# Second attention's output and the query projections as three rounded products, and late inputs split from the PSUM banks

## What is computed

```python
# first block, layer 0: differential attention, layer 1: stick-breaking attention
for i in range(DEPTH):
    h = rms_norm(x, norm1_g[i]) * (1.0 + sc1) + sh1
    y = diff_attention(h, ...) if i % 2 == 0 else stick_breaking_attention(h, sb_w_in, sb_w_out)
    x = x + g1 * y
    h = rms_norm(x, norm2_g[i]) * (1.0 + sc2) + sh2
    x = x + g2 * hierarchical_moe(h, ...)          # 32 experts, two for each token
x = rms_norm(x, final_norm_g)

def stick_breaking_attention(h, w_in, w_out):
...
    o = jnp.concatenate(outs, axis=1)
    return o.reshape(B, S, D) @ w_out

# second block, two layers
for l in range(DEPTH):
    h = h + hybrid_mixer(rms_norm_2(h, norm_mix[l]), ..., w_in[l], ..., w_out[l])
    h = h + memory_cross_attention(rms_norm_2(h, norm_xattn[l]), mem, norm_mem[l], wq[l], wk[l], wv[l], wo[l])

def memory_cross_attention(hn, mem, norm_mem, wq, wk, wv, wo):
    q = (hn @ wq).reshape(B, S, MEM_HEADS, MEM_HEAD_DIM)
    k = (memn @ wk).reshape(B, M, MEM_HEADS, MEM_HEAD_DIM)
...
    return o @ wo
```

## Time and the profile before

| | us |
|---|---|
| median of 3 runs | 2563.96 (2563.16 to 2566.67) |
| profiled execution, device time | 2564.52 |
| its span | 2562.7 |
| PE busy in it | 2279.2 (89%) |
| DVE busy | 1139.8 (44%) |
| ACT busy | 612.6 (24%) |
| POOL busy | 304.7 (12%) |
| mean granted TensorE clock | 0.951 of full speed |
| moved by DMA | 587.05 MB, mean 229 GB/s |

### The profile page before, as it was taken

One profiled execution on the slowest core, in us unless ns is written; L12 is line 12 of the kernel. 1 busy time (PEld: TensorE's weight loads), 2 busy tenths in 40 slices (PEclk: granted clock), 3 DMA queues, 4 the chain that ended last, 5 costly groups with the idle time before them and its releaser, 6 DMA issues.

```text
span 2562.7 us, 35298 instructions
## 1 busy us (share of the span) xinstructions
PE 2279.2 (89%) x13248; PEld 1517.4 (59%) x13248; DVE 1139.8 (44%) x2035; ACT 612.6 (24%) x1247; POOL 304.7 (12%) x555
## 2 busy tenths in 40 slices
PE   5988786999989869998799998985998999998997
PEld 3874464565545448654456454544786767786765
DVE  3236745334333342473533333335338525228615
ACT  3224520000000032461000000003336125226213
POOL 0001001222122210000122212221000000001000
PEclk8999897999999989999799999998999799999799
DMA  6247757999999942214799999994220021211021
GB/s 253 99 164 323 284 229 288 418 419 418 416 420 377 418 182 92 77 62 166 296 420 419 419 415 419 369 418 164 91 87 34 1 115 44 99 55 66 1 82 42
DMA packets 129177, 587.05 MB, mean 229 GB/s; under 512 B 28008, under 2 KB 28170, under 8 KB 72474
## 3 DMA queue, kind: packets, MB, share of 16 engines
q1 hardware_dynamic: 116704, 566.44, 55.2%
q0 software_dynamic: 12064, 16.87, 1.8%
q10 hardware_dynamic: 288, 2.10, 0.2%
HBM read 580.04 MB, written 27.30 MB: 237 GB/s over the span
## 4 chain that ended last, share of the span: by engine, by line
PE 70%; DVE 12%; DMA 12%; ACT 3%; issue 2%; POOL 1%; SPq 0%; DVEq 0%; ACTq 0%
PE banks L1397 15%; PE banks L1179 9%; PE banks L1180 9%; PE banks L1181 9%; PE banks L1415 8%; DMA normed_by_feature<-in_expert_w_up 6%; PE banks L1332 2%; PE banks L1210 2%; DVE normed_by_token L2344 2%; PE banks L1378 1%; PE banks L1101 1%; DMA scratch<-in_ada_w 1%; DMA weight_ring<-in_expert_w_up 1%; DMA weight_ring<-in_sb_w_in 1%; PE banks L1425 1%
## 5 line engine op out<-in xcount | busy, mean ns | idle before, releaser
L1397 PE MATMUL banks<-weight_ring,scratch 128*64 128x256 f32 x3328 | 381.5, 383 | 27.1 <-DMA weight_ring<-in_expert_w_gate 13.7
L1397 PEld LDWEIGHTS banks<-weight_ring,scratch 128*64 128x64 f32 x3328 | 238.9, 138 | 189.0 <-issue 53.9
L1179 PE MATMUL banks<-weight_ring_rounded,scratch_rounded 128*128 128x512 f32 x768 | 304.2, 396 | 8.3 <-DVE ormed_by_feature_rounded L2181 5.2
L1181 PE MATMUL banks<-weight_ring_rounded,scratch_rounded 128*128 128x512 f32 x768 | 300.6, 391 | 0.0
L1180 PE MATMUL banks<-weight_ring_rounded,ormed_by_feature_rounded 128*128 128x512 f32 x768 | 300.5, 391 | 0.0
L2168 DVE TENSOR_TENSOR weight_ring_rounded<-weight_ring,weight_ring_rounded 128x4096 fp32r<-128x4096 f32 x26 | 115.0, 4424 | 228.5 <-ACT weight_ring_rounded L1669 228.5
L1179 PEld LDWEIGHTS banks<-weight_ring_rounded,scratch_rounded 128*128 128x128 f32 x768 | 145.0, 189 | 47.1 <-issue 9.9
L1181 PEld LDWEIGHTS banks<-weight_ring_rounded,scratch_rounded 128*128 128x128 f32 x768 | 145.1, 189 | 30.8
L1415 PE MATMUL banks<-normed_by_token,scratch 128*64 128x512 f32 x640 | 146.1, 598 | 18.5 <-ACT scratch L1867 18.5
L1180 PEld LDWEIGHTS banks<-weight_ring_rounded,ormed_by_feature_rounded 128*128 128x128 f32 x768 | 145.1, 189 | 28.6
L1397 PE MATMUL banks<-normed_by_feature,scratch 128*64 128x256 f32 x1280 | 147.6, 381 | 15.9 <-DMA normed_by_feature<-in_expert_w_up 15.9
(11 more groups left out here) (391 smaller groups left out, 3437.0 us busy)
## 6 DMA issues: line engine op xcount, KB each, us to landing
weight_ring<-in_expert_w_gate SPq DMA_DIRECT2D x128, 1024.0 KB, 18.4
weight_ring<-in_expert_w_up SPq DMA_DIRECT2D x64, 1024.0 KB, 20.2
weight_ring<-in_expert_w_down SPq DMA_DIRECT2D x64, 1024.0 KB, 20.8
normed_by_feature<-in_expert_w_up SPq DMA_DIRECT2D x64, 1024.0 KB, 19.0
normed_by_token<-in_expert_w_down SPq DMA_DIRECT2D x64, 1024.0 KB, 19.1
weight_ring<-in_ada_w SPq DMA_DIRECT2D x20, 2048.0 KB, 12.1
weight_ring<-in_w_in SPq DMA_DIRECT2D x12, 2048.0 KB, 8.0
weight_ring<-in_diff_w_in SPq DMA_DIRECT2D x6, 2048.0 KB, 8.1
```

The costliest lines, as they stand in the source:

```text
L1179: pe.matmul(out_ap, left_high, right_high, start=i == 0, stop=False)
L1181: last = pe.matmul(out_ap, left_high, right_low, start=False, stop=i == len(turn_order(stage)) - 1)
L1397: last = pe.matmul(PS[ROWS * half:ROWS * (half + 1), 1 + n // 2, 0:HIDDEN // 2], XGT[:, j, h, :], w[:, j, HIDDEN // 2 * half:HIDDEN // 2 * ...
```

## The change

**Second attention's output.** attn_out of layer 1 becomes a split product with two weight units. Its high chunks are made in the stick loop by ACT, into a new buffer STICK_HIGH (in the tile of the projections); its low chunks by DVE behind the loop. Unit 0 is cast by ACT at j = 6 of qkv's last part (the V banks) and subtracted by DVE behind j = 5 there; unit 1 is done by both engines behind the stick loop. The banks are made in the order (0,0), (1,0), (0,1), (1,1), ... of token tile and half. The load of the memory stage's w_k for layer 1 moves from before the memory stage to behind the first 12 expert parts, and waits for the last bank of attn_out; w_v is now loaded ahead of w_k, and ACT's memory stage of layer 1 no longer waits for w_k.

**Query projections.** xq of both layers become split products. Their weights leave the ring: SP loads them into the tile of the projections once the mixer's output is mixed, ACT casts them at the head of its norm xattn, and DVE subtracts in mix_out, behind tile (1,1).

**Late inputs.** In norm mix, norm xattn, mtrans and xtrans, ACT writes the high chunk straight from the bank for all chunks, and DVE makes the low chunk from the same bank and the high one (`low_in_bank`). HT is no longer written in float32 there. PE waits for the bank to be drained where it waited for the low chunk.

**Moved.** The low half of project's first unit of layer 1 goes from the head of DVE's norm mix to x_out of layer 0, behind (1,1). attn_out of layer 1 now takes four loads of the ring instead of two and xq none instead of one, so the slots of what follows change.

```diff
-UNITS = {..., ("attn_out", 0): D // BANK,
+UNITS = {..., ("attn_out", 0): D // BANK, ("attn_out", 1): D // BANK,
+         ("xq", 0): 1, ("xq", 1): 1,
...
+def split_in_bank(stage):
+    return stage.kind in ("mtrans", "xtrans") or stage.kind == "norm" and stage.arg[0] in UNSCALED
...
+        QUERY_W, QUERY_HIGH, QUERY_LOW = (buf[:, SLOT * n:SLOT * (n + 1)].rearrange("p (k n) -> p k n", k=KD) for buf, n in ((BIGA, 1), (BIGA_R, 2), (BIGA_R, 1)))
+        STICK_HIGH = BIGA_R[:, 0:KD * S].rearrange("p (k s) -> p k s", k=KD)
...
-                    for n, w in enumerate((mem_wk_2, mem_wv_2)):
-                        sp.dma_start(MEM_W[n], by_row(w[layer], 0, BANK)).then_inc(memory_in, 16)
+                    for n, w in ((1, mem_wv_2), (0, mem_wk_2)):
+                        if n or layer == 0:
+                            sp.dma_start(MEM_W[n], by_row(w[layer], 0, BANK)).then_inc(memory_in, 16)
                 if stage.kind == "xq":
                     sp.wait_ge(mixed, MIXED * (stage.turn + 1))
                     sp.wait_ge(memory_stored, 16 * (layer + 1))
+                    sp.dma_start(QUERY_W, by_row(mem_wq_2[layer], 0, BANK)).then_inc(late_inputs_in, 16)
...
+                    if layer == 1:
+                        full_wait(sp, stage_of("attn_out", 1).fill + 7)
+                        sp.dma_start(MEM_W[0], by_row(mem_wk_2[layer], 0, BANK)).then_inc(memory_in, 16)
...
                 def chunk_ready(k):
                     pe.wait_ge(chunk_high, stage.splits_before + k + 1)
-                    pe.wait_ge(chunk_low, stage.splits_before + k + 1)
+                    if split_in_bank(before):
+                        drained_wait(pe, before.fill + k)
+                    else:
+                        pe.wait_ge(chunk_low, stage.lows_before + k + 1)
...
                 if stage.kind == "xq":
-                            last = pe.matmul(bank(n), w[:, k, j * P:(j + 1) * P], HT[:, k, :], start=k == 0, stop=k == KD - 1)
+                    pe.wait_ge(unit_low, stage.units_before + 1)
+                        split_fill(f0 + j, bank(f0 + j), lambda k: (w_high[:, k, cols], w_low[:, k, cols]), lambda k: (HT_HIGH[:, k, :], HT_LOW[:, k, :]))
...
-                elif stage.kind == "attn_out":
-                    w = [slot(u0 + h, BANK) for h in range(2)]
-                                last = pe.matmul(bank(n), HT[:, k, t * P:(t + 1) * P], w[half][:, k, :], start=k == 0, stop=k == KD - 1)
...
+                    elif stage.arg[0] == "xattn":
+                        act.wait_ge(late_inputs_in, 16 * (N_LATE + 2 * (stage.arg[1] + 1)))
+                        act.copy(QUERY_HIGH, QUERY_W).then_inc(act_prepared, 1)
...
+                        if split_in_bank(stage):
+                            full_wait(act, n)
+                            act.activation(HT_HIGH[:, k, :], bank(n), ACT.Identity, scale=gain[:, k:k + 1]).then_inc(chunk_high, 1)
+                            continue
...
+                        if layer and j == 6:
+                            unit_high(stage_of("attn_out", 1), 0)
...
+                            act.wait_ge(o_drained, c + 1)
+                            act.copy(STICK_HIGH[:, c, :], HT[:, c, :]).then_inc(chunk_high, 1)
+                    unit_high(product_after(stage), 1)
...
-                            drained(act.activation(HT[:, c, :], bank(n), ACT.Identity, scale=1.0), n)
-                            act.copy(HT_HIGH[:, c, :], HT[:, c, :]).then_inc(chunk_high, 1)
+                        act.copy(HT_HIGH[:, c, :], bank(f0 + i)).then_inc(chunk_high, 1)
...
+            def low_in_bank(product, k, at, n, gain):
+                dve.wait_ge(chunk_high, product.splits_before + at + 1)
+                if gain is None:
+                    drained(dve.tensor_tensor(HT_LOW[:, k, :], bank(n), HT_HIGH[:, k, :].bitcast(F32), ALU.subtract), n)
+                else:
+                    drained(dve.scalar_tensor_tensor(HT_LOW[:, k, :], bank(n), gain, HT_HIGH[:, k, :].bitcast(F32), ALU.mult, ALU.subtract), n)
...
-                    elif product and stage.arg not in (("first1", 1), ("mix", 0)):
-                        unit_low_half(product, 0)
...
+                        if layer and j == 5:
+                            unit_low_half(stage_of("attn_out", 1), 0)
...
+                    for c in range(KD):
+                        chunk_low_half(product_after(stage), c)
+                    unit_low_half(product_after(stage), 1)
...
+                                if (t, half) == (1, 1) and stage.kind == "mix_out":
+                                    dve.wait_ge(act_prepared, 4 + layer)
+                                    dve.tensor_tensor(QUERY_LOW, QUERY_W, QUERY_HIGH.bitcast(F32), ALU.subtract).then_inc(unit_low, 1)
+                                elif (t, half) == (1, 1) and layer < DEPTH - 1:
+                                    unit_low_half(product_after(stage, 2), 0)
```

More of the change, by code:

```diff
@@ L286, in plan_stages @@
         "project": [project_fills()["chunk", j, T - 1] for j in range(len(IN_CHUNKS))], "latent_up": [2 * T - 1, 4 * T - 1],
-        "mix_out": [6, 7], "xq": [XH - 1], "x_out": [7],
+        "mix_out": [6, 7], "x_out": [7],
     }
@@ L294, in plan_stages @@
         plan[-1].units_before = sum(stage.units for stage in plan[:-1])
-        plan[-1].splits_before = sum((XH if stage.kind == "x_out" else KD) for stage in plan[:-1] if stage.units)
+        splits = [(p, before, XH if p.kind == "x_out" else KD) for p, before in zip(plan, [None] + plan) if p is not plan[-1] and p.units]
+        plan[-1].splits_before = sum(n for _, _, n in splits)
+        plan[-1].lows_before = sum(n for _, before, n in splits if not split_in_bank(before))
         scaled += T if by_tile(kind, arg) else kind in ("norm", "memory", "final")
@@ L1300, in _ @@
                         fill_done(last, n)
-                if stage.kind in ("attn_out", "mix_out") and stage.units:
+                if stage.kind in ("attn_out", "mix_out"):
                     units = [unit_ready(0)]
@@ L1691, in _ @@
                 if stage.kind == "memory":
-                    act.wait_ge(memory_in, 48 * (layer + 1))
+                    act.wait_ge(memory_in, 48 * layer + (32 if layer else 48))
                     for t in range(MT):
@@ L2228, in _ @@
                         dve.wait_ge(dve_prepared, 2)
-                    elif product and stage.arg not in (("first1", 1), ("mix", 0)):
-                        unit_low_half(product, 0)
-                    for k in range(1, KD, 2):
+                    for k in range(KD):
                         n = f0 + k
+                        if split_in_bank(stage):
+                            low_in_bank(product, k, k, n, gain[:, k:k + 1])
+                            continue
+                        if k % 2 == 0:
+                            continue
                         full_wait(dve, n)
```

53 lines of the change are left out of this document (14 added, 39 removed).

## The result

| | before | changed |
|---|---|---|
| median, us | 2564.95 (2563.16 to 2566.67, 4 runs) | 2533.87 (2532.29 to 2534.83, 4 runs) |
| profiled execution / span | 2564.52 / 2562.7 | 2532.29 / 2530.4 |
| matmul records | 13248 | 13376 |
| granted clock | 0.951 | 0.951 |

The account below looks back on a forecast made before the run. PE, 70% of the chain of waits, was taken to bound the kernel. Savings of 11.5 + 11.4 + 2.8 + 4.0 + 2.6 + 4.3 = 36.6 us gave a median of 2527.4 us, range 2518 to 2543.

Parts of the forecast that it names:

- parts 1 and 2: Split products in layer 1's attention output and both layers' query projections: 11.5 and 11.4 us saved.
- the half-clock rival: Added rounded products run at half clock, shown by an average distance of 0.322 us: 40 us slower, 2604; chance 0.02.
- part 1, high chunks, "cost 0": Stick loop: eight ACT casts fit into ACT's 1.18 us free per head pair, DVE setting the pace at 9.24; cost 0.
- Unit 1 and w_k: Behind the stick loop, unit 1 ready with 1.5 us slack; w_k's load behind attn_out in an idle DMA stretch; cost 0.
- hidden work shows: Stick-loop casts (5.6 us), unit 1 late beyond its slack, or w_k ahead of expert loads (5.5): 2533 us; chance 0.15.
- part 3: Split from the bank at 0.69 us per instruction: norm mix 0 saves 2.8 us, mtrans 4.0, xtrans 2.6.
- The rival that it brings nothing: Bank split: hand-over between two engines costs what the SBUF pass cost; 21.0 us saved, 2543.0; chance 0.15.
- The estimate of 3.6 us from that page: Bank split: with 65 ns more for PSUM, subtractions take 0.75 us, outlast PE's 0.68, and lose some 3.6 us.
- part 4: Norm mix 1: unit's subtraction moved into x_out, PE's wait gone, first bank in 5.44 us: 4.3 us saved.
- part 5: Project 0's first load gets an earlier ring slot, but the queue is in order: 0 taken, 3.0 us at most.
- the forecast's own range: Whole kernel, 2522 to 2533 us, at chance 0.55.
- the stated one: Whole kernel, 2518 to 2543 us, including the bank rival, hidden work and slots, excluding half clock and upper ends.

Follow-up runs that it names:

- the two-pass kernel: Changed kernel with only the split from the bank undone, banks again going through HT in float32: 2546.3 us, ratio 0.9924 to the kernel before.
- the repeated trace: Trace of the changed kernel run again with nothing edited: 2532.75 us, ratio 0.9882 to the kernel before.

## Why the prediction was right, and where it missed

- **Products (parts 1 and 2).** Right: 11.14 of 11.5 for attention output, 5.66 and 5.68 of 5.7 for the queries, each confirmed by undoing it alone. The granted clock was 1.00 in both, so the half-clock rival, the one slower case, was wrong from its condition on: the pace was 0.2267, not over 0.322.
- **Cover in the stick loop (part 1, high chunks, "cost 0").** This step failed. It took DVE's 9.24 us as the pace of a pair and ACT's 1.18 us of waiting as free, and held the cast against that (0.45 to 0.69; it took 0.62, as ACT's rounding of 512 columns did in the trace of before, L1838: 620 ns). But the waiting was three waits of 0.24 to 0.47 us for PE, at fixed places in ACT's own round of 9.15 us. Against DVE's 9.24 that left 0.09, and the cast made the round 9.53. It cost 1.94 us in the compared traces, 1.1 in pairs at 9.5 and 0.8 behind the loop, where the cast of chunk 6 stands ahead of the last copies. How much it costs goes by ACT's lead at the start, 1.2 to 2.9 us in the eight traces. The rival "hidden work shows" had the right place at 5.6, two to five times its size.
- **Unit 1 and w_k.** Right. Unit 1 was ready at 1154.73, wanted at 1145.39 + 10.88 = 1156.27: 1.5 us ahead, the slack that was forecast. SP issued w_k at 1213.08 and the loop's first expert load at 1239.68; no wait of the chain names it. That load stands 50.8 us behind attention output's last matmul, before it was 51.1 (1248.21), so w_k pushed nothing. w_k was not tried in its old place, since the new chunk buffer lies there.
- **Split from the bank (part 3).** Right in price (0.60 to 0.74 forecast as 0.69) and in effect, 2.0 at the first banks where the clock was full. The rival that it brings nothing fell with the two-pass kernel, 12.5 us slower in its trace. The Trainium skill's 65 ns for reading PSUM in "Perfetto Trace Analysis", "Optimizing Scalar/DVE Operations", is not in DVE's rows: 682 ns from a bank, 688 from SBUF. (The estimate of 3.6 us from that page should have been 3.9: 56 chunks of 0.07.) And the Trainium skill's advice in "VectorE: DVE Perf Modes", "Rules for kernel authors", to copy out of PSUM first for many operations, does not yet hold for two, one on each engine.
- **Clock from project 0 to mix_out.** Missing from the sum: project 0's first bank (0.7, of which 0.6 is a half clock that lasted longer) and the mixer (1.0). Neither is the change's doing: the first bank took 5.55 us in the repeated trace, and the same mixer took from 166.0 us at a granted clock of 0.91 to 173.1 at 0.87 in the traces of the changed kernel and its variants. Together it was 1.7 of the 4.5 missing here.
- **Norm mix 1 (part 4).** Right: 2.39 of wait and late start gone, 2.09 in the first bank, 4.5 for 4.3. Of the 2.39, 1.85 is the unit's place. Of the 2.09, the two-pass kernel accounts for 1.3 (6.88 us at clock 1.00 there); the other 0.8 goes with the granted clock, 0.78 over that bank before and 1.00 in the changed kernel, and what raised it is not shown.
- **Ring slots (part 5).** Right at 0: the load took 28.8 us from its issue and landed 3.1 us behind the last expert matmul, as before (3.0).

```profile
1700.53 28.78 DMA weight_ring<-in_w_in
```

That is a row of the changed kernel's chain, for the earlier trace rows; the last expert matmul ends at 1726.25.

The 4.5 us between 36.6 and 32.1 are 1.9 of the loop, 1.7 from project 0 to mix_out and 1.0 that was there before the first changed instruction; the small differences of the other rows cancel. The measured median lies 1 us outside the forecast's own range and inside the stated one; it equals the 2533 of the rival by coincidence of two causes, one of which is not the rival's.

## What to carry to other kernels

Idle time of an engine in a loop is no cover as a sum: look at which wait it consists of, what it waits for, and how long the engine's own round is; then put the new instruction into a wait. The same cast two steps later lengthened no pair at full clock and left 0.3 us at the loop's end. When a product's input comes out of a bank, making each half from the bank saved a pass here, where one instruction per engine and chunk (0.67 us) stayed under the product's pace (0.68); no run shows it above that pace. And differences of a few us of a long kernel are read from distances between the same instructions in two traces, since single runs of one kernel scattered by up to 16 us here.

## What was not expected of the hardware

- The same kernel gave 2521.7 to 2537.6 us in one group of runs, with a mean granted clock of 0.953 and 0.947. One untouched stage, the mixer of layer 0, took from 166.0 to 173.1 us in the traces.
- PE kept busy with small matmuls through an idle stretch of 18 us kept its clock at 1.00 over the stretch and the transposes behind it, which the changed kernel's three traces ran at 0.50 to 0.71.
- DVE's subtraction from a bank with a gain for each partition takes 744 ns, without one 682; back to back eight of the first take 5.36 us, 0.67 each.
